# The first expert tiles of a hybrid diffusion step: list one-hots in memory of their own and made together, gates ahead of expert 1's splits, the second tile's transposes inside the first tile's up projection

## The reference, cut to what matters

```
pg = softmax(t @ w_rg)                      # 4 groups, the best one is taken
le = t @ w_re                               # 16 experts, 4 to a group
wt, idx = top_k(softmax(le of the group), 2)
gate = weights of the two experts, 0 for the rest
for e in range(16):
    a = silu(t @ w_eg[e]) * (t @ w_eu[e])   # 1024 -> 512, twice
    y = y + gate[:, e:e+1] * (a @ w_ed[e])  # 512 -> 1024
```

## Time and profile before

| what | value |
|---|---|
| median of 3 runs | 673.79 us (672.49 to 673.83) |
| the profiled execution | 672.04 us, its span 670.1 us |
| PE busy | 639.0 us, 95% of the span |
| DVE, ACT, POOL busy | 510.9, 416.0, 110.8 us |
| granted TensorE clock | 0.995 of full speed over the span |
| HBM | 280 GB/s over the span |
| chain that ended last | PE 77%, DVE 6%, DMA 6%, POOL 3% |

### The profile page before, as it was taken

The page is one execution under the profiler, slowest core; times in us unless marked ns, Lnnn a source line. Parts: engine busy times, 40 slices in busy tenths (PEclk is TensorE's granted clock), DMA queues, the critical chain, the costliest instruction groups (busy, mean ns, idle before and its releaser), DMA issues.

```text
span 670.1 us, 11052 instructions
## 1 busy us (share of the span) xinstructions
PE 639.0 (95%) x3570; PEld 524.3 (78%) x3570; DVE 510.9 (76%) x755; ACT 416.0 (62%) x640; POOL 110.8 (17%) x172
## 2 busy tenths in 40 slices
PE   2999999999999999999998899999999999999993
PEld 0577767889999998888786688888888888888872
DVE  2666576767676767775876988898989999899986
ACT  5552122344747486763445687888888888888873
POOL 2041000165000000000011650000000000290151
PEclk9999999999999999999999999999999999999997
DMA  9965768549212134495488799999999999999886
GB/s 332 386 244 184 264 242 254 156 148 336 64 34 59 62 101 151 147 324 189 159 313 320 251 336 419 419 420 420 420 420 420 420 420 419 416 403 376 320 308 157
DMA packets 77148, 188.16 MB, mean 281 GB/s; under 512 B 7824, under 2 KB 29381, under 8 KB 77109
## 3 DMA queue, kind: packets, MB, share of 16 engines
q1 hardware_dynamic: 65408, 153.11, 61.9%
q0 software_dynamic: 7392, 22.47, 9.8%
q10 hardware_dynamic: 4310, 12.10, 4.5%
HBM read 166.12 MB, written 21.53 MB: 280 GB/s over the span
## 4 chain that ended last, share of the span: by engine, by line
PE 77%; DVE 6%; DMA 6%; POOL 3%; ACT 2%; SPq 2%; issue 2%; POOLq 0%; ACTq 0%; DVEq 0%
PE ps L2128 20%; PE ps L2148 11%; PE ps L1839 10%; PE ps L1863 7%; PE ps L1895 6%; PE ps L1867 5%; PE ps L1916 3%; PE ps L1939 2%; PE ps L1772 2%; PE ps L2104 2%; SPq L462 2%; DMA catT_mem<-token_rows,rows_now 2%; PE ps L1930 2%; PE ps L1737 1%; DMA expert_rows<-catT_mem 1%
## 5 line engine op out<-in xcount | busy, mean ns | idle before, releaser
L2128 PE MATMUL ps<-split_ring,split_rows 128*128 128x512 f32 x720 | 168.3, 392 | 1.7 <-DVE split_rows L1568 1.0
L1485 DVE TENSOR_TENSOR split_ring<-qkv_mem,split_ring 128x1024 fp32r<-128x1024 f32 x124 | 144.0, 1221 | 23.4 <-ACT split_ring L970 23.2
L2128 PEld LDWEIGHTS ps<-split_ring,split_rows 128*128 128x128 f32 x720 | 133.9, 188 | 30.3 <-DVE split_ring L1485 1.6
L970 ACT CAST split_ring<-qkv_mem 128x1024 fp32r<-128x1024 f32 x124 | 121.1, 1053 | 9.3 <-ACT catT_mem L1076 9.3
L1863 PE MATMUL ps<-split_rows,split_ring 128*128 128x384 f32 x288 | 87.1, 349 | 0.2 <-ACT work L905 0.2
L2148 PE MATMUL ps<-split_ring,split_rows 128*128 128x512 f32 x360 | 86.3, 395 | 0.0
L2148 PEld LDWEIGHTS ps<-split_ring,split_rows 128*128 128x128 f32 x360 | 66.6, 188 | 13.6
L1867 PE MATMUL ps<-split_rows,split_ring 128*128 128x256 f32 x288 | 77.0, 280 | 0.0
L1485 DVE TENSOR_TENSOR split_ring<-raw_ring,split_ring 128x1024 fp32r<-128x1024 f32 x64 | 74.3, 1221 | 0.0
L1839 PE MATMUL ps<-split_ring,split_rows 128*128 128x512 f32 x288 | 68.0, 393 | 0.0
L970 ACT CAST split_ring<-raw_ring 128x1024 fp32r<-128x1024 f32 x64 | 62.4, 1046 | 0.9 <-DMA raw_ring<-in_w_exp_up 0.9
(11 more groups left out here) (361 smaller groups left out, 919.1 us busy)
## 6 DMA issues: line engine op xcount, KB each, us to landing
qkv_mem<-in_w_exp_gate SPq DMA_DIRECT2D x64, 512.0 KB, 8.3
qkv_mem<-in_w_exp_up SPq DMA_DIRECT2D x60, 512.0 KB, 7.0
raw_ring<-in_w_exp_down SPq DMA_DIRECT2D x60, 512.0 KB, 8.0
raw_ring<-in_w_mod SPq DMA_DIRECT2D x26, 512.0 KB, 4.5
qkv_mem<-in_w_mod SPq DMA_DIRECT2D x32, 256.0 KB, 7.0
expert_rows<-catT_mem ACTq DMA_DIRECT2D x14, 512.0 KB, 6.6
expert_rows<-work POOLq DMA_DIRECT2D x26, 256.0 KB, 5.9
raw_ring<-in_w_in SPq DMA_DIRECT2D x12, 512.0 KB, 6.4
```

The costliest lines, as they stand in the source:

```text
L970: nc.scalar.copy(moe_split(tile, j, r, 0), moe_raw(tile, j, r)).then_inc(S["hi"], 1)
L1485: tt(moe_split(tile, j, r, 1), moe_raw(tile, j, r), moe_split(tile, j, r, 0).bitcast(F32), ALU.subtract).then_inc(S["lo"], 1)
L2128: ins = mm(ps[:, j, :], rows[:, s, k * P:(k + 1) * P], moe_split(tile, j, k // 2, m)[:, (k % 2) * N:(k % 2 + 1) * N], start=(k == 0 and s ...
```

## The change

Five things move; no operation is added or taken away.

1. `list_oh` becomes ten places that touch no weights of expert 0 (eight in block 2 of part 0, two in part 1), and the wait for `g_mm` 1 goes. DVE does the list's comparisons ahead of both halves of `xT_lo((None, 0))` and the one-hots between the halves.
2. PE does `token_lists` ahead of `late_sums`, both right behind k = 0 to 3 of expert 0's gate.
3. DVE works out the gates right behind `steer`, ahead of the splits of expert 1's gate weights.
4. Quarter 3 of expert 1's gate weights is split into block 4 of `hs` and waits for `g_mm` 2 only; ACT splits it, and quarter 0 of expert 1's up weights, ahead of `xT_hi((None, 1))`. Inside expert 1, ACT puts `aT_hi` behind the up splits.
5. PE does `x_transposes((None, 1))` ahead of k = 6 and 7 of expert 0's up, and `a_transposes((None, 0))` behind k = 0 to 3 of expert 1's gate. DVE does `gated((None, 0))` between the halves of `xT_lo((None, 1))`.

```
+            if tile[0] is None and tile[1] == 1 and j == 0 and r == 3:
+                return hs[:, part, CTX * D:(CTX + 1) * D]
...
-        list_oh = hs[:, 0, 2048:3328].rearrange("p (m s) -> p m s", m=2 * TB)
+
+        def list_oh(m):
+            o = 2048 + m * P if m < 8 else 2400 + (m - 8) * P
+            return hs[:, 0 if m < 8 else 1, o:o + P]
...
-                    elif tile[0] is None and j == 0 and moe_split_slot(tile, j, r) == FIRST_ROWS:
-                        act.wait_ge(S["u_mm"], 4)
+                    elif tile[0] is None and j == 0 and r == 3:
+                        act.wait_ge(S["g_mm"], BLOCKS.index(CTX) + 1)
...
+                else:
+                    split_expert(tile, 1, (1, 2, 3))
+                    aT_hi((tile[0], tile[1] - 1))
...
-            split_expert((None, 1), 0, (2,))
+            split_expert((None, 1), 0, (2, 3))
+            split_expert((None, 1), 1, (0,))
             xT_hi((None, 1))
-            split_expert((None, 1), 0, (3,))
...
-            xT_lo((None, 0), (0,))
...
             link(stt(spot, rw["in"], -float(P), rw["sl"], ALU.mult, ALU.add))
+            xT_lo((None, 0), (0,))
+            for m in range(2 * TB):
+                ins = ts(list_oh(m), count, spot[:, m:m + 1], 1.0, ALU.subtract, ALU.is_equal)
+            ins.then_inc(S["lists_in"], 1)
             xT_lo((None, 0), (1,))
-            dve.wait_ge(S["g_mm"], 1)
-            for m in range(2 * TB):
-                ins = ts(list_oh[:, m, :], count, spot[:, m:m + 1], 1.0, ALU.subtract, ALU.is_equal)
-            ins.then_inc(S["lists_in"], 1)
...
-            split_lo_moe((None, 1), 0, (0,))
-            gated((None, 0))
-            xT_lo((None, 1))
-            split_lo_moe((None, 1), 0, (1, 2, 3))
...
             tt(gate[:, 1, :], gate[:, 0, :], rw["e2"], ALU.mult).then_inc(S["steer_ready"], 1)
+            split_lo_moe((None, 1), 0, (0, 1))
+            xT_lo((None, 1), (0,))
+            gated((None, 0))
+            xT_lo((None, 1), (1,))
+            split_lo_moe((None, 1), 0, (2, 3))
...
             gate_up((None, 0), (0,), range(4))
+            token_lists()
             late_sums()
-            gate_up((None, 0), (0,), range(4, 6))
-            token_lists()
-            gate_up((None, 0), (0,), range(6, KC))
+            gate_up((None, 0), (0,), range(4, KC))
             pe.wait_ge(S["row_copied"], 1)
-            gate_up((None, 0), (1,))
+            gate_up((None, 0), (1,), range(6))
             x_transposes((None, 1))
+            gate_up((None, 0), (1,), range(6, KC))
+            gate_up((None, 1), (0,), range(4))
             a_transposes((None, 0))
-            gate_up((None, 1))
+            gate_up((None, 1), (0,), range(4, KC))
+            gate_up((None, 1), (1,))
```

More of the change, by code:

```diff
@@ L1090, in expert_tile @@
                     split_expert(tile, 0)
-                aT_hi((tile[0], tile[1] - 1))
-                if tile[0] is not None:
+                    aT_hi((tile[0], tile[1] - 1))
                     out_rows((tile[0], tile[1] - 2))
-                split_expert(tile, 1)
+                    split_expert(tile, 1)
+                else:
+                    split_expert(tile, 1, (1, 2, 3))
+                    aT_hi((tile[0], tile[1] - 1))
                 gate_act(tile)
@@ L2109, in token_lists @@
                 for m in range(2 * TB):
-                    ins = mm(list_ps, list_oh[:, m, :], list_val[:, m, :], start=(m == 0), stop=(m == 2 * TB - 1))
+                    ins = mm(list_ps, list_oh(m), list_val[:, m, :], start=(m == 0), stop=(m == 2 * TB - 1))
                 ins.then_inc(S["list_mm"], 1)
@@ L2115, in late_lists @@
                 for m in range(2 * TB):
-                    ins = mm(late_ps, list_oh[:, m, :], late_val[:, m, :], start=(m == 0), stop=(m == 2 * TB - 1))
+                    ins = mm(late_ps, list_oh(m), late_val[:, m, :], start=(m == 0), stop=(m == 2 * TB - 1))
                 ins.then_inc(S["list_mm"], 1)
```

## The result

The changed kernel takes 669.41 us in the median (668.44 to 670.32, 6 runs), the one before 673.40 (672.00 to 676.18, 6 runs). The ratio is 0.9942, with a 95% interval of 0.9921 to 0.9964: about 3.9 us faster. Two later comparisons of the same program gave 0.9962 [0.9948, 0.9976] and 0.9943 [0.9924, 0.9963].

What follows compares the result with a forecast made beforehand. PE was taken as the bound, so only its gaps count: waits of 5.53 us less 1.15 left gain 4.4, taking 672.04 to 667.6, plus 1.75 for the median gives 669.4 us; range 667.3 to 671.9.

Steps and rivals of the forecast that it cites:

- the base, 673.79: Whole kernel before the change: profiled execution of 672.04 us, with the median of the runs 1.75 above it.
- PE is the bound, and an entry gain goes through whole: Loop and tail: PE busy 230.00 of 230.00 us from 403 to 633, so an entry gain reaches the tail whole.
- The first tile's gate costs nothing: Tile 0's gate: list operations ahead of the first half of `xT_lo` cost nothing, at most 0.1 us.
- Gather issued at 356.67, landing as before in 7.52 us, wait 0.95: Tile 1's transposes: gather issued 2.57 us earlier lands at 364.19, so PE waits 0.95 us instead of 2.18.
- the same loads around it: Tile 1's gather: reason for keeping 7.52 us; DMA share of this stretch 0.87, against 1.02 in the loop.
- the gather is slower: Rival at tile 1's gather: with 10 us, wait 3.4, gain 1.9, time 671.9; chance 0.13 for gain 0 to 3.4.
- the idle time of about 1 us: Sign of being right: PE's idle time ahead of tile 1's transposes falls to about 1 us.
- the short end: Tile 1's gather: engines taking packets in turn from the queues speaks for short landings; shortest of 13 later gathers 7.1 us.
- The last six up matmuls cover the rows' split, wait 0.1: Ahead of expert 1's gate: 1.4 us of expert 0's up fills the split; wait 0.1 us instead of 0.96.
- Expert 1: 0.25 us of room in up: Expert 1's up: quarter 0 split at 372.65, wanted at 372.9; wait 0 instead of 0.71 us.
- Late lists and tile 3: waits gone: POOL's chain starts at 363.1, takes 8.7 us; waits of 1.24 (late lists) and 0.44 us (tile 3's transposes) go.
- The loads keep up: Weight loads: DMA follows a PE 4.4 us ahead; tightest room 4.3 us, so loss at most 0.1 us.

Runs made afterwards that it cites:

- e5: Changed kernel with SP holding the four loads of expert 0's down weights until tile 1's gather has landed; ratio to the kernel before 0.9936, entry 47.03 us.
- e11: The same kernel as e5, run again without further edit; ratio to the kernel before 0.9920, median 667.91 us, entry 47.04 us.
- e4: Changed kernel with tile 1's transposes put back behind all of expert 0's up projection; ratio to the kernel before 0.9952, entry 48.20 us.
- e10: Changed kernel with POOL's two modulation-row operations and their DMAs moved right behind the issue of the first gathers; ratio to the kernel before 0.9924, entry 47.46 us.
- e3: Kernel before with only the early lists: list operations around the first tile's rows, list matmuls ahead of the late sums; ratio 0.9990, entry 51.48 us.
- e9: e5 with POOL's two modulation-row operations and their DMAs moved right behind the issue of the first gathers; ratio to the kernel before 0.9938, median 670.07 us.
- e1: Changed kernel run again with no edit; ratio to the kernel before 0.9962, entry 48.62 us.
- e6: Changed kernel with POOL holding tile 2's gather until tile 1's has landed; ratio to the kernel before 0.9967, entry 50.17 us.
- e12: Changed kernel run a third time with no edit; ratio to the kernel before 0.9943, entry 48.24 us.
- e2: Kernel before with only the gates worked out right behind steer, ahead of the splits of expert 1's gate weights; ratio 0.9970, entry 49.35 us.
- e7: Changed kernel with both expert 0's down loads and tile 2's gather held until tile 1's gather has landed; ratio to the kernel before 0.9928, entry 47.12 us.
- e8: e5 with tile 1's transposes put behind all of expert 0's up projection; ratio to the kernel before 0.9933, entry 47.00 us.

## Why the prediction was right, and where it was not

The time, 669.41, and the forecast, 669.4, agree better than the reasoning deserves. The forecast gain was 4.4 us, the entry shows 3.44; the base, 673.79, was 0.4 above the median of the later runs, and the three ratios mean 2.6 to 3.9 us. That two terms that were too small in the sum, the gather and DVE's splits, were in part made up by busy time that it did not count is luck.

*PE is the bound, and an entry gain goes through whole.* Right. 226.00 of 226.00 us busy in the loop after, and the last tile's down projection starts 3.7 us earlier than before (630.13 against 633.84).

*The first tile's gate costs nothing.* Right: PE's first gate matmul starts at 350.88 without a wait ahead of it, the half of `xT_lo` having ended at 350.77.

*Gather issued at 356.67, landing as before in 7.52 us, wait 0.95.* **This is the step that failed.** Issued at 356.43, it landed in 8.7 to 8.9 us in every profiled execution of the early lists with the loads free, and PE waited 2.3 to 2.5 us for it where the transposes stand inside the up: 1.4 us too little in the sum. I argued with "the same loads around it"; but issued 2.8 us earlier it meets the end of expert 1's up loads and the first down loads together, and holding the down loads back brings it to 5.1 (e5) and 5.9 us (e11). So the rival "the gather is slower" is what happened, at 8.8 and not 10 us, and of the signs that I gave the idle time of about 1 us did not come.
The fit of the Trainium skill ("DMA: Bandwidth & Descriptors", Anatomy of one DMA), 3.2 us as an estimate, was reached nowhere; 5.1 was the shortest. That engines take turns between queues (same page, Queues, rings and completion order) I had read as speaking for the short end; the trace disagrees, for q0 moved nothing for 4.0 us while q1 moved 1.6 MB.

*The last six up matmuls cover the rows' split, wait 0.1.* Right in itself (no wait at 367.83), but worth nothing, by e4: the sum counted the cover and, through the gather's forecast, not its price.

*Expert 1: 0.25 us of room in up.* Half right. The room was there by the lengths that I used; what I had not counted is that POOL's work, now 17 us earlier, stretches DVE's splits. It showed as a wait of 0.22 us and cost 0.76, by e10.

*Late lists and tile 3: waits gone.* Right. POOL's chain began at 363.09, forecast 363.1. Its length was wrong: 3.8 us to 366.91, not 8.7, with the room larger for it.

*The loads keep up.* Right: from 350 on to the end of the loop the profile shows no engine waiting for a weight load.

The sum then reads: waits 5.53 before, 2.59 after, 2.94 us gone, and the entry 3.44 shorter. The other 0.50 us is in the busy times: the last matmul ahead of a wait counts in full, 0.39 us, while within a run the next one starts 0.23 us after it. Expert 1's up takes 5.74 us before, where a wait follows, and 5.57 now from its start to that of the late lists (374.65 to 380.22); the 48 matmuls ahead of tile 3's transposes took 11.18 us (391.10 to 402.28) and take 11.02 (388.06 to 399.08). Where a matmul ends is modelled by the profile, so a part of this may belong to the waits. It is argued from the rows, not tried.

Which part did it? The gates alone bring 2.3 of the 3.4 us in the entry (0.5 of it a lucky gather). The lists alone bring 0.2, having won 1.1 us at the gather; but that one execution holds the clock dip of 1.75 us, and over all runs of e3 the ratio's interval reaches from 0.5 us slower to 1.8 us faster. The transposes' new place brings nothing as long as the gather is late. Whether the remainder needs the parts together, or is what the dip hides, stays open.

## What to carry to other kernels

An operation that another engine's chain hangs on should stand ahead of everything that waits for a transfer: six small instructions moved past a wait were worth 2 us. A transfer that is issued earlier may also meet more traffic, so its old duration is no price for the new place; holding bulk loads that nobody wants for ten more microseconds, behind the small one that is wanted now, is one line and was worth 1.1 us in the entry. And after a gap is closed ask what the engines in the shadow now do at the same time; here POOL's idle-time work slid onto DVE's critical splits.

## What the runs showed of the hardware

**DVE and POOL hold each other up, both ways.** POOL's chain of small operations takes 8.7 us beside DVE's splits, each operation about 1.1 us, the length of a split. In the changed kernel, with DVE waiting for tile 1's rows, the same operations take 0.2 to 0.3 us:

```profile
363.09 2.35 POOL L706 TENSOR_SCALAR work<-work 128x10 f32<-128x10 f32 x2 [3.30 <-DVE small L1637]
365.52 0.23 POOL L707 TENSOR_TENSOR work<-small,work 128x20 f32<-128x20 f32 x1
365.83 0.23 POOL L708 TENSOR_TENSOR split_rows<-iota_consts,work 128x20 fp32r<-128x20 f32 x1
366.00 0.22 POOL L709 CAST split_rows<-work 128x20 fp32r<-128x20 f32 x1
...
366.91 0.36 POOL L712 TENSOR_SCALAR work<-work 128x10 f32<-128x10 f32 x1
```

The other way round, a split goes from 1.21 to 2.3 us (e5, and the changed kernel) and a tiny operation from 0.31 to 1.66 (e9). The Trainium skill states a rule for this ("SBUF — State Buffer", Who interferes with whom): a DVE instruction with two SBUF inputs and a GpSimd instruction that reads SBUF exclude each other for a whole instruction. The runs agree: a 34 x 512 operation on POOL takes 1.29 us, and the split beside it 1.1 us longer. Read against the change ahead of time, it would have flagged the two 34 x 512 operations that slide onto expert 1's splits.

**The granted clock sometimes falls behind a wait.** The windows of e1, where PE had waited 2.32 us up to 364.9 (columns as in the earlier trace rows; the third number from the end is the granted clock):

```profile
366.00:370.00 4.00, 4.00 (x13) 3.14 (x12) 2.23 (x4) 3.91 (x5) 3.49 (x8) 0.57 0.65 243
370.00:374.00 4.00, 4.00 (x21) 3.30 (x20) 3.92 (x4) 0.59 (x1) 3.47 (x6) 1.00 0.31 73
```

of e3, behind its wait of 1.24 us for the late lists, and of e9, behind its 2.38 us:

```profile
382.00:386.00 4.00, 4.00 (x21) 3.71 (x22) 1.88 (x3) 1.15 (x4) 3.59 (x6) 0.63 1.00 399
```

```profile
368.00:372.00 4.00, 4.00 (x12) 3.05 (x12) 3.20 (x4) 0.04 (x1) 3.62 (x7) 0.61 1.00 388
```

and of the changed kernel's first execution, which had waited 2.37 us:

```profile
366.00:370.00 4.00, 3.98 (x19) 3.02 (x19) 2.77 (x4) 3.53 (x5) 3.40 (x10) 1.00 0.75 268
```

A mean clock of 0.57 over 4 us means the lower level, 1.2 GHz, for most of the stretch. It came in e1, e3, e6 and e9, after single waits of 1.24 to 2.38 us with other waits ahead of some, and did not come in the changed kernel's first execution, e10 and e12 with waits of the same length, nor in e2, e4, e5, e7, e8 and e11. It costs up to 1.75 us (e3). In e1 two rows take 1.5 us longer for it, and 1.1 us of that comes back, since DVE's stretched splits are then on time. The dip may be part of why times of one program scatter. What decides whether it comes stays open.
